# Causal attention: both heads of a pair scored together, one head's mask on DVE, constant products in the fill, one value bank

## What is computed

```
def _masked_softmax(s, mask):
    s = jnp.where(mask, s.astype(jnp.float32), -jnp.inf)
    m = jnp.max(s, axis=-1, keepdims=True)
    ...
    p = jnp.exp(s - m)
    return p / jnp.maximum(jnp.sum(p, axis=-1, keepdims=True), 1e-30)
...
ps = _masked_softmax(jnp.einsum('bgrqd,bgqkd->bgrqk', qc, kg) * scale, (kpos <= tpos[:, None])[:, :, None])
osl = jnp.einsum('bgrqk,bgqkd->bgrqd', ps.astype(vg.dtype), vg)
...
return gc[..., 0:1] * oc + gc[..., 1:2] * osl + gc[..., 2:3] * ow
```

## Time and profile before

| | |
|---|---|
| three runs, us | 3270.03, 3285.07, 3287.79 (median 3285.07) |
| profiled execution, us | 3267.99, its span 3266.2, mean granted clock 0.896 |
| PE busy | 2748.4 us (84% of the span) |
| DVE busy | 1703.7 us (52%) |
| ACT busy | 1079.5 us (33%) |
| the stage, first score product to last `turn` | 2394.2 to 2556.4 us of the span |

### The profile page before, as it was taken

The page is one execution under the profiler, slowest core; times in us unless marked ns, Lnnn a source line. Parts: engine busy times, 40 slices in busy tenths (PEclk is TensorE's granted clock), DMA queues, the critical chain, the costliest instruction groups (busy, mean ns, idle before and its releaser), DMA issues. The chain is left out here.

```text
span 3266.2 us, 41926 instructions
## 1 busy us (share of the span) xinstructions
PE 2748.4 (84%) x15966; PEld 2125.7 (65%) x15966; DVE 1703.7 (52%) x2643; ACT 1079.5 (33%) x1788; POOL 91.9 (3%) x101
## 2 busy tenths in 40 slices
PE   7979899756658999998968999957799847599998
PEld 4634887645346788786637888846666636478886
DVE  3535222677554588637976877342224362454432
ACT  3322101354212555324334554221124210245531
POOL 0034000000000000000000000000000000000000
PEclk9989999966878999999988999978769967699999
DMA  8723132001014233421112333222100100223332
GB/s 294 248 81 129 52 84 58 13 4 47 7 52 135 65 97 96 112 62 52 51 30 61 102 97 95 80 58 76 52 7 1 47 1 2 65 78 96 96 98 71
DMA packets 374147, 240.99 MB, mean 74 GB/s; under 512 B 8048, under 2 KB 345840, under 8 KB 374000
## 3 DMA queue, kind: packets, MB, share of 16 engines
q1 hardware_dynamic: 374000, 238.96, 24.6%
HBM read 236.31 MB, written 2.10 MB: 73 GB/s over the span
## 5 line engine op out<-in xcount | busy, mean ns | idle before, releaser
L1086 DVE SCALAR_TENSOR_TENSOR ffn_acc<-ffn_pad,cols_sb,ffn_acc 128x512 f32<-128x512 f32 x380 | 263.7, 746 | 32.6 <-ACT ffn_acc L1013 32.6
L223 PE MATMUL bank<-ffn_x_high,pre_high 128*128 128x512 f32 x528 | 212.2, 402 | 14.2 <-DVE ffn_x_low L475 10.7
L224 PE MATMUL bank<-ffn_x_low,pre_high 128*128 128x512 f32 x528 | 210.6, 399 | 0.0
L225 PE MATMUL bank<-ffn_x_high,pre_low 128*128 128x512 f32 x528 | 210.6, 399 | 0.0
L223 PE MATMUL bank<-ffn_x_high,ffn_w_high 128*128 128x512 f32 x528 | 205.5, 389 | 0.0
L225 PE MATMUL bank<-ffn_x_high,ffn_w_low 128*128 128x512 f32 x528 | 205.5, 389 | 0.0
L224 PE MATMUL bank<-ffn_x_low,ffn_w_high 128*128 128x512 f32 x528 | 205.4, 389 | 0.0
L223 PE MATMUL bank<-ffn_h_high,ffn_down_w_high 128*128 128x512 f32 x480 | 190.3, 397 | 0.0
L224 PE MATMUL bank<-ffn_h_low,ffn_down_w_high 128*128 128x512 f32 x480 | 189.6, 395 | 0.0
L225 PE MATMUL bank<-ffn_h_high,ffn_down_w_low 128*128 128x512 f32 x480 | 188.7, 393 | 0.0
L1307 DVE SCALAR_TENSOR_TENSOR conf_u<-conf_pad,cols_sb,conf_u 128x512 f32<-128x512 f32 x162 | 121.8, 752 | 16.9 <-ACT conf_u L1274 11.7
(11 more groups left out here) (734 smaller groups left out, 6388.0 us busy)
## 6 DMA issues: line engine op xcount, KB each, us to landing
ada_ring<-in_ada_w SPq DMA_DIRECT2D x48, 1024.0 KB, 7.0
pre_ring<-in_ffn_w_up SPq DMA_DIRECT2D x88, 512.0 KB, 3.9
pre_ring<-in_ffn_w_in SPq DMA_DIRECT2D x44, 512.0 KB, 3.9
ffn_down_ring<-in_ffn_w_down SPq DMA_DIRECT2D x28, 704.0 KB, 4.7
ffn_down_ring<-in_ffn_w_out SPq DMA_DIRECT2D x14, 704.0 KB, 4.5
pre_ring<-in_conf_w SPq DMA_DIRECT2D x18, 512.0 KB, 5.0
f_ring<-in_mix_w_in SPq DMA_DIRECT2D x32, 256.0 KB, 3.0
mix_out_ring<-in_mix_w_out SPq DMA_DIRECT2D x16, 512.0 KB, 3.9
```

Source lines behind the costliest of these rows:

```text
L223: pe.matmul(bank, weights[0], acts[0], start=start, stop=False)
L224: pe.matmul(bank, weights[0], acts[1], start=False, stop=False)
L225: return pe.matmul(bank, weights[1], acts[0], start=False, stop=stop)
L1086: dve.scalar_tensor_tensor(out=dst, in0=src, scalar=conv_w(2 * i + j, n), in1=dst, op0=ALU.mult, op1=ALU.add).then_inc(tapped[j], 1)
```

## The change

In PE's list the two heads of a query tile are scored one behind the other, into four score banks, and only head 0 gets its mask by a product. Head 1 gets it by a DVE addition in the bank, and its maximum waits for that addition. The loops now go by query tile (q, 36 of them): PE runs both `turn` of q, then `scores(q + 2)`; ACT both exponentials of q, then both `take` of q - 2; DVE the two maxima of q, then `finish(q - 1)`. Two query tiles are scored ahead, followed by four 128x512 products of constants into the bank of `count`. Values use one bank instead of two, and `count` and `lift` move by a step.

```
--- before.py
+++ after.py
@@ -2717,14 +2717,15 @@
     ends = {p: n for p, (n, _) in enumerate(pairs) if p + 1 == len(pairs) or pairs[p + 1][0] != n}
     units = [(p, t, e) for p in range(len(pairs)) for t in QUERY_ORDER for e in range(2)]
     n_u, n_t = len(units), len(tiles)
-    depth, lag = 6, 4
+    n_q = n_u // 2
+    depth, lag = 6, 2
...
+        def score_bank(u):
+            return banks[u % 4]
+
+        def by_pe(e):
+            return e == 0
+
+        scored = [scored0, scored1]
+
         @block.tensor
         def _(pe):
-            def scores(u):
-                p, t, e = units[u]
+            def scores(q):
+                p, t, _ = units[2 * q]
                 branch = pairs[p][1]
-                rows = slice(HD * e, HD * e + HD)
-                if u >= 3:
-                    pe.wait_ge(exp_done, u - 2)
-                pe.matmul(banks[u % 3][:, 0:width(u)], branch.q[rows, t * P:(t + 1) * P], branch.k[rows, 0:width(u)],
-                          start=True, stop=False)
-                pe.matmul(banks[u % 3][:, t * P:(t + 1) * P], ident[:, :], masked[:, :], start=False, stop=True)\
-                  .then_inc(scored, 1)
+                if q >= 2:
+                    pe.wait_ge(exp_done, 2 * (q - 1))
+                for e in range(2):
+                    rows = slice(HD * e, HD * e + HD)
+                    mm = pe.matmul(score_bank(2 * q + e)[:, 0:width(2 * q)], branch.q[rows, t * P:(t + 1) * P],
+                                   branch.k[rows, 0:width(2 * q)], start=True, stop=not by_pe(e))
+                    if not by_pe(e):
+                        mm.then_inc(scored[e], 1)
+                for e in range(2):
+                    if by_pe(e):
+                        pe.matmul(score_bank(2 * q + e)[:, t * P:(t + 1) * P], ident[:, :], masked[:, :], start=False, stop=True)\
+                          .then_inc(scored[e], 1)
 
             def turn(u):
                 pe.wait_ge(scaled, u + 1)
                 if u >= 2:
                     pe.wait_ge(taken, u - 1)
                 for n in range(units[u][1] + 1):
-                    mm = pe.matmul(banks[3 + u % 2][:, n * P:(n + 1) * P], prob[:, u % depth, n * P:(n + 1) * P],
+                    mm = pe.matmul(banks[4 + u % 2][:, n * P:(n + 1) * P], prob[:, u % depth, n * P:(n + 1) * P],
                                    diag[:, u % depth, :], start=True, stop=True)
                 mm.then_inc(turned, 1)
 
             def values(p):
                 n_tile, branch = pairs[p]
-                bank = banks[5 + n_tile % 2]
+                bank = banks[6]
                 first = p == 0 or pairs[p - 1][0] != n_tile
                 cmp_pair = tiles[n_tile][2]
                 pe.wait_ge(taken, UNITS * (p + 1))
-                if first and n_tile >= 2:
-                    pe.wait_ge(lifted, n_tile - 1)
+                if first and n_tile >= 1:
+                    pe.wait_ge(lifted, n_tile)
...
@@ -2784,16 +2798,21 @@
             def after(u):
                 if u >= UNITS + 1 and u % UNITS == 1:
                     values(u // UNITS - 1)
-                if u % UNITS == 2 and u // UNITS - 2 in ends:
+                if u % UNITS == 3 and u // UNITS - 2 in ends:
                     count(ends[u // UNITS - 2])
 
             pe.wait_ge(masks_in, 2)
-            for s in range(n_u + lag):
-                if s < n_u:
-                    scores(s)
-                if s >= lag:
-                    turn(s - lag)
-                    after(s - lag)
+            for q in range(lag):
+                scores(q)
+            for n in range(4):
+                pe.matmul(banks[7][:, :], core.const("ident"), core.const_sb[:, 0:TT, :].rearrange("p n q -> p (n q)"),
+                          start=True, stop=True)
+            for q in range(n_q):
+                for e in range(2):
+                    turn(2 * q + e)
+                if q + lag < n_q:
+                    scores(q + lag)
+                after(2 * q + 1)
...
@@ -2815,7 +2834,7 @@
                 if p >= 2:
                     act.wait_ge(summed, p - 1)
                 act.activation(prob_t[:, p % 2, e, 0:t + 1, t * P:(t + 1) * P],
-                               banks[3 + u % 2][:, 0:width(u)].rearrange("k (n q) -> k n q", q=P), ACT.Copy).then_inc(taken, 1)
+                               banks[4 + u % 2][:, 0:width(u)].rearrange("k (n q) -> k n q", q=P), ACT.Copy).then_inc(taken, 1)
 
             def square(n_tile):
                 act.wait_ge(lifted, n_tile + 1)
...
-            for s in range(n_u + lag):
-                if s < n_u:
-                    act.wait_ge(top_done, s + 1)
-                    if s >= depth:
-                        act.wait_ge(turned, s - depth + 1)
-                    act.activation(probs(s), banks[s % 3][:, 0:width(s)], ACT.Exp, bias=top[:, s:s + 1],
-                                   accum_out=total[:, s:s + 1]).then_inc(exp_done, 1)
-                if s >= lag:
-                    u = s - lag
-                    take(u)
+            for q in range(n_q + lag):
+                if q < n_q:
+                    for u in (2 * q, 2 * q + 1):
+                        act.wait_ge(top_done, u + 1)
+                        if u >= depth:
+                            act.wait_ge(turned, u - depth + 1)
+                        act.activation(probs(u), score_bank(u)[:, 0:width(u)], ACT.Exp, bias=top[:, u:u + 1],
+                                       accum_out=total[:, u:u + 1]).then_inc(exp_done, 1)
+                if q >= lag:
+                    for u in (2 * (q - lag), 2 * (q - lag) + 1):
+                        take(u)
                     if u % UNITS == 7 and u // UNITS - 1 in ends:
                         square(ends[u // UNITS - 1])
             square(n_t - 1)
@@ -2861,17 +2881,24 @@
 
             def lift(n_tile, p):
                 dve.wait_ge(summed, p + 1)
-                dve.tensor_copy(mix[:, tiles[n_tile][0], :], banks[5 + n_tile % 2][:, :]).then_inc(lifted, 1)
+                dve.tensor_copy(mix[:, tiles[n_tile][0], :], banks[6][:, :]).then_inc(lifted, 1)
 
             dve.tensor_copy(ident[:, :], core.const("ident")).then_inc(masks_in, 1)
             dve.tensor_copy(masked[:, :], core.const("neg_since")).then_inc(masks_in, 1)
-            for u in range(n_u):
-                dve.wait_ge(scored, u + 1)
-                dve.tensor_reduce(top[:, u:u + 1], banks[u % 3][:, 0:width(u)], AX_X, ALU.max, negate=True).then_inc(top_done, 1)
-                if u >= 3 and u % 2 == 1:
-                    finish((u - 3) // 2)
-                if u % UNITS == 1 and u // UNITS - 2 in ends:
-                    lift(ends[u // UNITS - 2], u // UNITS - 2)
+            for q in range(n_q):
+                t = units[2 * q][1]
+                for e in range(2):
+                    u = 2 * q + e
+                    dve.wait_ge(scored[e], q + 1)
+                    if not by_pe(e):
+                        last = score_bank(u)[:, t * P:(t + 1) * P]
+                        dve.tensor_tensor(last, last, core.const("neg_since"), ALU.add).then_inc(masked_out, 1)
+                        dve.wait_ge(masked_out, q + 1)
+                    dve.tensor_reduce(top[:, u:u + 1], score_bank(u)[:, 0:width(u)], AX_X, ALU.max, negate=True).then_inc(top_done, 1)
+                if q:
+                    finish(q - 1)
+                if 2 * q % UNITS == 0 and 2 * q // UNITS - 2 in ends:
+                    lift(ends[2 * q // UNITS - 2], 2 * q // UNITS - 2)
             finish(n_u // 2 - 1)
             for p in (len(pairs) - 2, len(pairs) - 1):
                 if p in ends:
```

More of the change, by code:

```diff
@@ L2724, in causal_attention @@
             core.split_room(att_mask=[P, P]) as ((ident, masked),), \
-            core.stage("masks_in", "scored", "top_done", "exp_done", "guarded", "inverted", "gated", "scaled", "turned", "taken",
+            core.stage("masks_in", "scored0", "scored1", "masked_out", "top_done", "exp_done", "guarded", "inverted", "gated", "scaled", "turned", "taken",
                        "summed", "lifted", "squared", "counted", "var_done", "root_done", "root_inverted", "spread_done", "normed") as (
-                block, masks_in, scored, top_done, exp_done, guarded, inverted, gated, scaled, turned, taken, summed, lifted,
+                block, masks_in, scored0, scored1, masked_out, top_done, exp_done, guarded, inverted, gated, scaled, turned, taken, summed, lifted,
                 squared, counted, var_done, root_done, root_inverted, spread_done, normed):
```

## The result

The changed kernel takes 3324.33 us (median of 4 runs, 3319.65 to 3331.81), the kernel before 3286.43 us (median of its 4 runs by then, 3270.03 to 3302.73). The ratio is 1.0131, 95% interval 1.0094 to 1.0167: about 43 us slower. The profiled executions differ by 53.6 us (3321.61 against 3267.99).

A forecast was written before the change was run, and what follows sets the result against it. The prediction held PE to be the bound. A waiting loop at half clock, 239.5 us of stage, 77 over before, less 5, made 72 us slower: 3340 us, 3357 on the median's footing, 3350 predicted, range 3292 to 3395.

The forecast's parts named there:

- PE is the bound, DVE and ACT have slack: Stage before the change: PE busy 160.4 of 162.2 us, DVE and ACT working only 68 and 71 us.
- the prediction's count of PE's work: PE's stage work at full clock, 110 us; the rival with gaps still covered, 52 us saved, had chance 0.07.
- The two heads overlap: Neighbouring score products in two row halves cost one head's time, 2.95 us per branch; no overlap had chance 0.10.
- The closed loop: PE must wait for `turn(q)` behind DVE's and ACT's work on q + 1; 10.5 us per branch.
- The chain: Mask's start for q + 1 to start of `turn(q)`: 2.0 us for the narrowest scores to 3.2 for the widest.
- the way over `take`: Wait of `turn` through exponential and `take` on ACT, held a little longer than the way over `finish`, which it hides.
- At full clock 7 us slower: Stage with the loop's waits but no clock loss: 169.5 us against 162.2; mostly full clock had chance 0.14.
- The clock falls in every branch and comes back with the values: Waits drop PE to 1.2 GHz, back for a few us at most; 72 us slower, chance 0.57 for mostly half clock.
- I take 5 off for the stretches that values and constants keep fast: Allowance for full-clock stretches: 5 us off the half-clock stage's excess of 77 us, leaving 72 us slower.
- On the median's footing: Median runs lie 17 us above the profiled execution, so 3340 us becomes 3357; 3350 was predicted.
- Edits at nothing: One value bank, four score banks and the constants cost nothing; the constants up to 3.5 us if the clock is down.
- The signs: Profile after: some 30 waits for `take`, 2 to 3 us each, clock 0.5 to 0.65; wrong if PE above 90% busy.

The follow-up runs named there:

- e1: Changed kernel with scores of query tile q + 2 ahead of both turns of q in PE's list; 3226.44 us, ratio 0.9853, stage 118.6 us.
- e9: Changed kernel with ACT's list going exponential, take, exponential, take; 3314.34 us against 3269.80 before, stage 207.5 us.
- e2: Changed kernel, order kept, plus filler products of constants on PE behind every pair of scores; 3289.93 us against 3271.22 before, stage 177.7 us.
- e4: Changed kernel without the four products of constants in the fill; 3325.33 us against 3271.22 before, stage 214.0 us.
- e5: Kernel before the change, with four products of constants added ahead of the fourth unit's scores; 3271.10 us against 3286.89, stage 168.8 us.
- e6: Changed kernel with scores ahead of turns and without the products of constants; 3224.01 us against 3286.89 before, stage 116.8 us.
- e11: Changed kernel with scores ahead of turns, both masks on PE, takes between exponentials, no constants; 3222.37 us, ratio 0.9842, stage 115.0 us.
- e8: Changed kernel with scores ahead of turns and both heads' masks on PE; 3224.09 us against 3286.89 before, stage 115.9 us.
- e10: Changed kernel with scores ahead of turns and each take behind one exponential on ACT; 3220.79 us against 3269.80 before, stage 114.2 us.
- e7: Changed kernel with scores ahead of turns and head 0's mask product between the two heads' scores; 3262.86 us against 3286.89 before, stage 151.4 us.

## Why the prediction was right, and where it was off

- **PE is the bound, DVE and ACT have slack.** Right; in the open order PE is busy for 110.9 of 119.0 us, against the 110 of the prediction's count of PE's work.
- **The two heads overlap.** Right: two heads of 512 columns reached their mask in 1.06 us at full clock in the fill (2391.54 to 2392.60, above), where one head took 1.05. The trace agrees with the Trainium skill, page "TensorEngine Tiling (Array Packing)", section "Key Properties", that tiles compute in parallel. The warning in its "PSUM Bottleneck" section fits the changed kernel in that saved PE time turned into waiting, but e1 shows that the order of PE's list, not the speed of the evacuation, was at fault.
- **The closed loop.** Right in place and size. The chain measured 3.30 us for the widest scores, against 3.2, and the addition 0.32, against 0.32. e1 takes the loop away and with it the loss. The prediction held the way over `take` to be the longer one, by 0.8 us a branch; at the widest scores it was, by at least 0.2 us, and e9, where the exponentials and so the diagonal matrices come later, won 0.6 us a branch.
- **At full clock 7 us slower.** The sum was 169.5 us. e2, near full clock but with its own fillers, came to 177.7. That the loop loses with hardly any fall of the clock is shown (177.7 against 162.0); how much of the 8 us above the sum the fillers make is open. The changed kernel gives an estimate of its own, under the next point, of 168.
- **The clock falls in every branch and comes back with the values.** The fall is right: 15 stretches at 1.2 GHz in nine branches. **The size of the clock's part was the term that failed.** "I take 5 off for the stretches that values and constants keep fast": all at half clock the sum was 239.5 us, and the stage took 212.9, so 27 us came off, not 5. Only 112.6 of the 213 us were at 1.2 GHz, and the granted clock was 0.74 where the prediction expected 0.5 to 0.65. One branch, and the sum over all 15 half-clock stretches (their bounds rounded to 0.1 us):

```profile
2425.90:2432.70 6.80, 5.16 (x32) 2.43 (x30) 3.68 (x15) 3.36 (x11) 0.00 (x0) 1.00 0.00 0
2432.70:2436.10 3.40, 3.01 (x14) 2.81 (x16) 0.47 (x2) 0.42 (x3) 0.00 (x0) 0.50 0.00 0
2436.10:2439.50 3.40, 1.29 (x5) 0.39 (x5) 1.97 (x6) 1.19 (x3) 0.00 (x0) 1.00 0.00 0
2439.50:2449.80 10.30, 7.64 (x31) 6.56 (x33) 2.18 (x11) 2.58 (x10) 0.00 (x0) 0.50 0.00 0
...
sum 112.80, PE 90.17 PEld 74.56 DVE 22.33 ACT 24.22 POOL 0.00; mean PE 6.01 PEld 4.97 DVE 1.49 ACT 1.61 POOL 0.00
```

  The clock came back twice in this branch. The first time was at 2425.9, behind the four-block turns and the 384-wide scores and ahead of the compressed values (2426.15) and the values (2427.15); the second at 2436.1, behind the three-block turns and in the 512-wide scores, with no values near. So "with the values at most" was wrong. PE did 90 of its 155 busy us at half clock; at full clock those would take 45, so half clock cost at most 45 us, where the prediction had 65 (239.5 less 169.5 less 5). It also puts the loop at full clock at 168 us or more, an estimate, against the sum of 169.5.
- **On the median's footing.** The forecast 3350 lay half-way between the profile's footing and the median's. The stage grew by 51 us in place of 72, and the medians differ by 38, the ratio gives 43. The 8 to 13 us between these are those of the kernel before: its median here lies 18 us above its profile, that of the changed kernel 3 us above its own. Why its executions differ so is open, as only one was profiled. The 10 us that the forecast added for this footing had no counterpart; most of the 26 us between 3350 and 3324.33 are the stage's clock.
- **Edits at nothing.** Right for the constants (e4: 1.1 us). No wait of PE in the stage is named for `lift` (L2884), which frees the single value bank.
- **The signs.** PE was busy 73% of the stage, under the 90% that would have spoken against the prediction, and the pair took one head's time. The waits for `take` that were to come some 30 times, 2 to 3 us each, are named 15 times in the profile; 17 more are named for the diagonal matrices.

## What to carry to other kernels

When a pipeline is regrouped in pairs, draw for each engine what stands directly ahead of the instruction that the bound engine waits for: the same "lag" counted in pairs can be a step less of cover, and here one moved call (scores ahead of turns, not behind) was worth 94 us of stage time. A saving on the bound engine that makes it wait is paid for twice if its clock falls with the waits, as it did here. Ahead of adding filler work to hold a clock, look for an order that leaves no gap: fillers won back 35 us, the order 94.

## What the runs showed of the hardware that was not expected

TensorE's clock fell in work without a pause. In e5 it fell at 2490.7 us behind a `count` (eight passes with two moving columns each, 0.95 us) between two 256-wide score products of 64 rows, then stayed at half for 20.5 us of unbroken scoring and turning, until values ran:

```profile
2487.05 0.70 PE L2743 MATMUL bank<-nsa_q 64*128 64x256 f32 x2
...
2488.12 0.95 PE L2780 MATMUL bank<-const_sb,att_sq 128*128 128x2 f32 x8
2489.00 0.70 PE L2743 MATMUL bank<-nsa_q 64*128 64x256 f32 x2
...
2490.15 1.59 PE L2743 MATMUL bank<-moba_qk 64*128 64x512 f32 x2
2491.68 0.47 PE L2745 MATMUL bank<-att_mask_low,att_mask_high 128*128 128x128 f32 x1
```

The 512-wide score product that began at 2490.15 took 1.53 us to its mask, between the 1.05 and 2.00 of the two levels. So PE's busy time alone does not tell whether the clock holds. Nor does the order of the products: in the profile of the kernel before the same `count` stands between the same 256-wide scores, with the same 512-wide ones behind it, and the clock held:

```profile
2502.93 0.95 PE L2780 MATMUL bank<-const_sb,att_sq 128*128 128x2 f32 x8
```

```profile
2501.80:2511.00 9.20, 9.01 (x49) 5.90 (x45) 4.20 (x15) 4.45 (x15) 0.00 (x0) 1.00 0.00 0
```

What decides it is not shown. In the five open orders with both heads' scores side by side the clock fell at most once, for 3.4 to 6.8 us (e1, e6, e11), or not at all (e8, e10); with the heads apart 30.7 us were at half clock (e7), and 41.0 and 47.8 in the kernel before and e5. Each is one execution.
